# Attention with the split probabilities as stationary operands and v with columns of ones moving

## The chip, the cores and the metric

The kernel runs on one NeuronCore of a Trainium2 chip. The metric is the time of one execution on the device in microseconds (us); lower is better. The kernel before takes 1997.43 us, the median of three runs (1996.18 to 1998.01).

## What is computed

A trunk of two residual layers over 1,024 tokens of width 1,024, in 4-byte floats. Layer 0 has two attention groups of 8 heads each, layer 1 one of 16:

```python
for i in range(DEPTH):                       # DEPTH = 2
    u = rms_norm(h, norm_g[i])
    if i % 2 == 0:                           # mla: 8 heads, q and k of 96, v of 64; chk: 8 heads of 64
        o_a = mla_attention(...)             # block-causal softmax over chunks of 64
        o_b = chunk_rel_attention(...)       # own chunk and 8 before it, with a position bias
        mixed = concat([o_a * silu(g_a), o_b * silu(g_b)]) @ ab_w_out
    else:                                    # fox: 16 heads of 64
        o_c = forgetting_attention(...)      # causal softmax with a cumulative forget bias
        mixed = (o_c * silu(g_c)) @ fox_w_out
    h = h + mixed
    h = h + (p[i] @ pe_w[i]) * sigmoid(rms_norm(h, pe_gate_norm[i]) @ pe_gate_w[i])
```

Every attention is `softmax(q k^T * scale + mask or bias) @ v`, per head.

## The kernel before

The program is a chain of stages with a barrier between them: `stage_ab` (norms, projections), `stage_attention` three times (mla, chk, then after `stage_oe("m")` fox), `stage_oe("t")` at the end. Stages hand data over through DRAM (`s_q`, `s_v`, `s_g` and others); the attention stages leave their gated outputs in SBUF as `a_hi` and `a_lo`, features on partitions. A value is kept as a sum of two parts of reduced precision (`hi`, `lo`, type fp32r), and a product is computed as hi·hi + hi·lo + lo·hi.

In `stage_attention` a head has NT = 8 query tiles of 128, and a tile t looks at key blocks `lowest(t)` to t, that is t + 1 blocks, in chk at most 5. The five instruction streams are written out by hand, in steps s = 8 · head + t:

- TensorE, step s: `score(s)` fills one of two PSUM areas (two matmul terms per piece of up to 512 keys, three in mla; a mask is added by a small bf16 matmul); `times_v` for a *pair* of query tiles, half of it in an even and half in an odd step; `turn_p(s - 2)` transposes the probabilities of tile s - 2 in pieces of up to 4 blocks, two pieces in flight; in even steps `spread_sums`, two transposes that bring 1/sum onto all partitions.
- ScalarE: `exp(s)` with the row sum in `accum_out`; `evacuate(s - 2)` copies each transposed piece to `pt_hi`; `take_far` copies P·v and the inverses out of PSUM.
- VectorE: `row_max(s)` (in chk bias and maximum in one custom operation); `invert`; `evacuate(s - 2)` computes `pt_lo`; `take_o` adds the half of P·v that stands on its own 64 partitions to the half in `far`.
- GpSimd: gate and inverse multiplied in (`gi`, `o`) and `a_lo` split, three operations of 1,024 columns per pair of heads; for the last pair VectorE does them.
- The DMA queue of SyncE: q, k, their low parts, v and the gate, a head ahead, each load of q and k whole.

In P·v a block of v is stationary (L1050): a head's 128 columns of v are [hi | lo] or, in odd heads, [lo | hi], and `pt_hi`, then `pt_lo` move, 256 columns of them where both tiles of the pair see the block:

```python
cols = slice(P, 2 * P) if j == 2 * u + 1 else slice(0, P) if j < lo1 else slice(0, 2 * P)
ins = nc.tensor.matmul(pv[:, uu % 2, 0, cols], v[:, b, j, :], part[:, u % 2, j - lo0, cols],
                       start=(m == 0), stop=(m == len(terms) - 1))
```

The first score term uses all 128 rows of the array (96 in mla). The second (L1009) uses `XROWS`: 64 in chk, 67 in fox (three rows carry the forget bias), 96 in mla.

The gate projection (units "g" in `stage_ab` L652 and `stage_oe("m")` L1595) has the weights stationary and 512 tokens moving, 24 matmuls per unit, 16 units in each stage; all other projections have tokens stationary and 256 weight columns moving.

Of the kernel before, what the change touches and what calls it, by code (L numbers as in the profile page):

```python
# [55 lines left out]
def build(nc, x, p, positions, norm_g, ab_w_in, mla_q_norm, mla_w_uq, mla_kv_norm, mla_w_ukv,  # L56
# [12 lines left out]
    s_g = dram("s_g", [FH, 64, S])  # L69
# [5 lines left out]
    f_g = dram("f_g", [FH, 64, S])  # L75
# [122 lines left out]
    def stage_ab():  # L198
        with ExitStack() as st:
# [86 lines left out]
            for u, (kind, c, n) in enumerate(units):  # L286
# [9 lines left out]
                if kind == "qk":  # L296
                    steps.append(("b", u))
# [67 lines left out]
            pair_g = s_g.rearrange("(c h) q n -> c (h q) n", h=2)  # L365

            with nc.Block() as block:

                @block.sync
                def _(sync):  # L370
# [39 lines left out]
                    for what, n in steps:  # L410
# [11 lines left out]
                        if what == "e" and ("e", n) in outs_at:  # L422
# [10 lines left out]
                            else:  # L433
                                m = c - G0
                                pair = (4 + 2 * m if m < 2 else 2 * m - 4) + t // 2
                                store(o, pair_g[pair, :, (t % 2) * HALF:(t % 2 + 1) * HALF], src[:, 0:HALF])
# [19 lines left out]
                def _(act):  # L456
# [20 lines left out]
                    def evacuate(u):  # L477
# [3 lines left out]
                        if ("e", u) in outs_at:  # L481
# [7 lines left out]
                            if kind == "g":  # L489
                                nc.scalar.activation(staged[:, o % 4, 0:HALF], src[:, 0, :], ACT.Silu).then_inc(out_made, 1)  # L490
                                return
# [76 lines left out]
                def _(pe):  # L568
# [47 lines left out]
                    def unit(u, part):  # L616
# [16 lines left out]
                        elif kind == "qk":  # L633
# [11 lines left out]
                        elif kind == "v":  # L645
                            last = tokens(dst[:, 0:256], c, n, a_hi, a_lo, 0, 256)
                        else:
                            w_hi, w_lo = wt.halves(c)
                            block, cols = slice(n // 2 * P, (n // 2 + 1) * P), slice(n % 2 * HALF, (n % 2 + 1) * HALF)
                            for k in range(KD):  # L650
                                for w, a in ((w_hi, a_hi), (w_hi, a_lo), (w_lo, a_hi)):
                                    last = nc.tensor.matmul(dst, w[:, k, block], a[:, k, cols],  # L652
                                                            start=(k == 0 and w is w_hi and a is a_hi),
                                                            stop=(k == KD - 1 and w is w_lo))
# [219 lines left out]
    def stage_attention(kind, heads, first_pair, q_of, k_of, v_of, g_of, extra_of):  # L874
# [3 lines left out]
        NU = NT // 2  # L878
# [7 lines left out]
        def turned(t):  # L886
# [5 lines left out]
        BEFORE = [sum(len(turned(t)) for t in range(n)) for n in range(NT + 1)]  # L892

        def piece(s):

            return BEFORE[NT] * (s // NT) + BEFORE[s % NT]

        def in_units(rows):
            return rows.rearrange("q (u n) -> q u n", u=NU)

# [874 lines left out]
```

## Time and profile before

| | us |
|---|---|
| median of three runs | 1997.43 |
| the profiled execution | 1996.7 |
| its span, first to last instruction | 1994.9 |
| stage mla, first score to last split | 160.1 |
| stage chk | 167.2 |
| stage fox | 295.6 |

The profile is a record of one execution. For each engine it has the start and the duration of every instruction and what ended the idle time before it. Over the whole span TensorE is busy 1783.1 us in matmuls and 1637.5 us in loads of stationary operands (these two overlap), VectorE 955.8, ScalarE 827.3 and GpSimd 98.3 us. The end of a matmul is modelled, and one starts before the one ahead of it ends; so its cost in a stream is the distance from its start to the next start, and the duration says little. The granted clock (PEclk) is a share of TensorE's 2.4 GHz. In the rows, PE is a matmul, PEld a load of the stationary operand, DVE VectorE, ACT ScalarE, POOL GpSimd, SPq the DMA queue; `out<-in rows*columns` gives the tensors and the part of the array; L and a number is the line of the kernel. A row of a window has the stretch (from:to), its length, the busy us of each engine with its number of instructions (x), the granted clock, the share of the DMA engines and their GB/s.

### The profile page before, as it was taken

The numbers are of one execution on the slowest core, as the hardware profiler recorded it, in microseconds if no ns is written. First come the engines' busy times: TensorE is split into PE (matmuls) and PEld (weight loads), VectorE is DVE, ScalarE is ACT, GpSimd is POOL, SyncE is SP. The second block draws the span as 40 slices with busy tenths as digits, with TensorE's granted clock in tenths as the row PEclk, the third lists the DMA queues.
The fourth block names the chain that finished last, engine by engine and source line by source line (L and its number), as shares of the span: only waits on it lengthen the run. The fifth ranks groups of instructions, "written<-read, shape, count | busy, mean of one in ns | idle before, by whom it ended". The sixth has DMA issues, their size and how long they took to land. (4 is left out here: it accounts for less than half of the span.)

```text
span 1994.9 us, 31875 instructions
## 1 busy us (share of the span) xinstructions
PE 1783.1 (89%) x12720; PEld 1637.5 (82%) x12720; DVE 955.8 (48%) x1797; ACT 827.3 (41%) x1702; POOL 98.3 (5%) x55
## 2 busy tenths in 40 slices
PE   5999778988996996999989999999968988869998
PEld 5999767867884775999988999998757777769898
DVE  5454556105774665234345444331057777722631
ACT  4433234215773675123153332312157878711410
POOL 0000000000210111000000000000002112100000
PEclk9999989998996998999999999999989999989999
DMA  5054468416424551510123433453174555251111
GB/s 179 22 197 143 119 160 220 122 56 171 127 75 111 138 129 42 184 54 27 49 106 106 127 123 119 131 138 102 45 178 122 142 138 129 64 180 48 64 64 38
DMA packets 178372, 223.94 MB, mean 112 GB/s; under 512 B 12857, under 2 KB 148297, under 8 KB 178225
## 3 DMA queue, kind: packets, MB, share of 16 engines
q1 hardware_dynamic: 177152, 218.43, 38.1%
q0 software_dynamic: 640, 2.62, 0.4%
q8 instruction: 102, 1.67, 0.4%
q10 hardware_dynamic: 432, 0.85, 0.1%
q14 instruction: 46, 0.37, 0.1%
HBM read 150.34 MB, written 77.29 MB: 114 GB/s over the span
## 5 line engine op out<-in xcount | busy, mean ns | idle before, releaser
L1562 PE MATMUL m_acc<-m_w_hi,g_a_hi 128*128 128x256 f32 (+1 forms) x1280 | 370.6, 290 | 19.0 <-DVE m_w_lo L179 14.6
L1562 PE MATMUL m_acc<-m_w_hi,g_a_lo 128*128 128x256 f32 (+1 forms) x1280 | 365.5, 286 | 0.0
L1562 PE MATMUL m_acc<-m_w_lo,g_a_hi 128*128 128x256 f32 (+1 forms) x1280 | 364.6, 285 | 0.0
L1562 PEld LDWEIGHTS m_acc<-m_w_hi,g_a_hi 128*128 128x128 f32 x1280 | 246.0, 192 | 19.4 <-DVE m_w_lo L179 14.7
L1562 PEld LDWEIGHTS m_acc<-m_w_lo,g_a_hi 128*128 128x128 f32 x1280 | 246.8, 193 | 0.0
L1562 PEld LDWEIGHTS m_acc<-m_w_hi,g_a_lo 128*128 128x128 f32 x1280 | 244.6, 191 | 0.0
L611 PE MATMUL pa_acc<-pa_w_hi,g_a_hi 128*128 128x256 f32 (+2 forms) x512 | 156.4, 305 | 15.9 <-DVE pa_w_lo L179 15.9
L1562 PE MATMUL t_acc<-t_w_hi,g_a_hi 128*128 128x256 f32 x512 | 146.9, 287 | 15.2 <-DVE t_w_lo L179 15.2
L611 PE MATMUL pa_acc<-pa_w_hi,g_a_lo 128*128 128x256 f32 (+2 forms) x512 | 151.8, 297 | 0.0
L611 PE MATMUL pa_acc<-pa_w_lo,g_a_hi 128*128 128x256 f32 (+2 forms) x512 | 151.5, 296 | 0.0
L1562 PE MATMUL t_acc<-t_w_hi,g_a_lo 128*128 128x256 f32 x512 | 145.6, 284 | 0.0
L1562 PE MATMUL t_acc<-t_w_lo,g_a_hi 128*128 128x256 f32 x512 | 144.9, 283 | 0.0
L1150 DVE TENSOR_TENSOR fox_pt_lo<-fox_turn,fox_pt_hi 128x128 fp32r<-128x128 f32 (+2 forms) x192 | 100.3, 550 | 59.5 <-ACT fox_pt_hi L1086 58.2
L1024 PE MATMUL fox_turn<-g_ident,fox_prob 128*128 128x128 f32 x576 | 90.8, 280 | 31.1 <-DVE fox_pt_lo L1150 29.9
L611 PEld LDWEIGHTS pa_acc<-pa_w_hi,g_a_hi 128*128 128x128 f32 x512 | 99.6, 195 | 16.4 <-issue 16.4
L1562 PEld LDWEIGHTS t_acc<-t_w_hi,g_a_hi 128*128 128x128 f32 x512 | 97.7, 191 | 15.3 <-DVE t_w_lo L179 15.3
L1086 ACT ACTIVATE fox_pt_hi<-fox_turn 128x128 fp32r<-128x128 f32 (+2 forms) x192 | 87.2, 489 | 47.5 <-PE fox_turn L1024 45.3
L1136 DVE TENSOR_REDUCE fox_neg_max<-fox_scores 128x1 f32<-128x128 f32 (+7 forms) x128 | 95.6, 747 | 17.1 <-PE fox_scores L1009 16.4
L1075 ACT ACTIVATE fox_prob<-fox_scores,fox_neg_max 128x128 f32<-128x128 f32 (+7 forms) x128 | 94.8, 741 | 20.1 <-DVE fox_neg_max L1136 20.0
L611 PEld LDWEIGHTS pa_acc<-pa_w_lo,g_a_hi 128*128 128x128 f32 x512 | 100.0, 195 | 0.0
L611 PEld LDWEIGHTS pa_acc<-pa_w_hi,g_a_lo 128*128 128x128 f32 x512 | 99.0, 193 | 0.0
L1562 PEld LDWEIGHTS t_acc<-t_w_lo,g_a_hi 128*128 128x128 f32 x512 | 98.4, 192 | 0.0
(284 smaller groups left out, 4136.4 us busy)
## 6 DMA issues: line engine op xcount, KB each, us to landing
m_w_raw<-in_fox_w_in SPq DMA_DIRECT2D x16, 1024.0 KB, 6.0
pa_w_raw<-in_ab_w_in SPq DMA_DIRECT2D x10, 1024.0 KB, 5.6
f_v<-m_pr SPq DMA_DIRECT2D x32, 256.0 KB, 2.8
fox_q<-f_q SPq DMA_DIRECT2D x32, 256.0 KB
fox_k<-f_k SPq DMA_DIRECT2D x32, 256.0 KB
fox_v<-f_v SPq DMA_DIRECT2D x16, 512.0 KB, 3.3
s_mq<-pa_xr SPq DMA_DIRECT2D x32, 192.0 KB, 3.0
s_mk<-pa_xr SPq DMA_DIRECT2D x32, 192.0 KB, 3.1
```

What stands on the lines that cost most here:

```text
L611: last = nc.tensor.matmul(dst, a[:, k, t * P:(t + 1) * P], w[:, k, n0:n0 + n], start=(k == 0 and a is m_hi and w is w_hi), stop=(k == kt - ...
L1024: last = nc.tensor.transpose(turn[:, g % 2, m, :], prob[:, s % 3, (j - lo) * P:(j - lo + 1) * P], ident[:])
L1075: nc.scalar.activation(prob[:, s % 3, 0:n], src, ACT.Exp, bias=neg_max[:, s % 4:s % 4 + 1], scale=-1.0 if chk else 1.0, accum_out=total[:, ...
L1086: nc.scalar.activation(pt_hi[:, u % 2, at:at + len(js), (s % 2) * P:(s % 2 + 1) * P], turn[:, g % 2, 0:len(js), :], ACT.Copy).then_inc(pt_ ...
L1136: nc.vector.tensor_reduce(r, scores[:, t % 2, 0:n], AX_X, ALU.max, negate=True).then_inc(maxed, 1)
L1150: nc.vector.tensor_tensor(pt_lo[where], turn[:, g % 2, 0:len(js), :], pt_hi[where].bitcast(F32), ALU.subtract).then_inc(pt_lo_done, 1)
L1562: last = nc.tensor.matmul(dst, a[:, k, t * P:(t + 1) * P], w[:, k0 + k, 0:n], start=(k == 0 and a is m_hi and w is w_hi), stop=(k == kt - ...
```

## The change

The roles in P·v are swapped. A transposed block of probabilities (`pt_hi`, then `pt_lo`) is stationary, and v moves: 130 columns [lo | hi | 1 1] against `pt_hi`, 66 columns [hi | 1 1] against `pt_lo`. Each query tile is a unit of its own, and P·v comes out with queries on partitions, with the row sum in column 128. VectorE inverts that sum and takes the outputs, scaled; GpSimd adds the two halves and multiplies by the gate for four tiles at once; TensorE turns the outputs by four transposes per half of a head pair, and ScalarE and VectorE split them into `a_hi` and `a_lo` from PSUM. The spreading of sums, `accum_out` and `far` go.

With it come: gates with tokens on partitions (`s_g`, `f_g`), so that the gate projection has tokens stationary and is done in two parts of 256 columns like the others; the second score term over all 128 rows in chk and fox, with zeros that GpSimd fills in at the start of the stage; v loaded into rows of 130; the first head's q and k loaded in two halves of the tokens, v between them; PSUM areas chosen by s instead of t. The core of the diff ("..." marks what is left out):

```diff
-    s_g = dram("s_g", [FH, 64, S])
+    s_g = dram("s_g", [KD, P, ST, P])
...
-        return blocks[:, :, 1:3, :] if small else blocks[:, :, 0::3, :]
+        return blocks[:, :, 0::2, :] if small else blocks[:, :, 1::2, :]
...
-                if kind == "qk":
+                if kind in ("qk", "g"):
                     steps.append(("b", u))
...
-                        elif kind == "qk":
+                        elif kind in ("qk", "g"):
                             last = tokens(dst[:, part * 256:(part + 1) * 256], c, 2 * n + part, a_hi, a_lo, 0, 256)
...
-                            for k in range(KD):
-                                for w, a in ((w_hi, a_hi), (w_hi, a_lo), (w_lo, a_hi)):
-                                    last = nc.tensor.matmul(dst, w[:, k, block], a[:, k, cols],
...
-            XROWS = QK if mla else 67 if fox else 64
+            VCOLS = P + 2
...
-            v = sp.sb("v", [P, 2, ST, P], F32R)
-            gate = sp.sb("gate", [P, 2, S])
-            gi = sp.sb("gi", [P, S])
-            far = sp.sb("far", [P, 2, NU, 2, 2 * P])
+            v = sp.sb("v", [P, 2, ST, VCOLS], F32R)
+            gate = sp.sb("gate", [P, 2, ST, P])
+            o_parts = sp.sb("o_parts", [P, 2, ST, 2, 64])
+            o_sum = sp.sb("o_sum", [P, 4, 64])
+            pt_hi = sp.sb("pt_hi", [P, 3, WIDE // P, P], F32R)
+            pt_lo = sp.sb("pt_lo", [P, 3, WIDE // P, P], F32R)
...
+                        if hd == 0:
+                            load_v(0)
+                            load_qk(0, slice(HALF, S), in_rest)
...
+                        if s == NT // 2:
+                            pe.wait_ge(in_rest, 16 * QKDMA)
...
-                                ins = nc.tensor.matmul(dst, a[0:r, b, rows], kk[0:r, b, keys], start=(m == 0),
+                                ins = nc.tensor.matmul(dst, a[0:KROWS, b, rows], kk[0:KROWS, b, keys], start=(m == 0),
...
+                    def turn_o(g):
+                        _, m, half = ring[g]
+                        pe.wait_ge(gated, 4 * m + 2 + half + 1)
+                        turn_ready(g)
+                        for n in range(4):
+                            last = nc.tensor.transpose(turn[:, g % 2, n, :], o[:, m % 2, 4 * half + n, :], ident[:])
...
-                    def spread_sums(uu):
...
+                        wait(pe, taken, s - 1)
+                        pe.wait_ge(pt_lo_done, p_upto[s])
+                        for j in range(lo, t + 1):
+                            nc.tensor.matmul(pv[:, s % 2, 0:VCOLS], pt_hi[:, s % 3, j - lo, :], v[:, b, j, :],
+                                             start=(j == lo), stop=False)
+                            ins = nc.tensor.matmul(pv[:, s % 2, 64:VCOLS], pt_lo[:, s % 3, j - lo, :], v[:, b, j, 64:VCOLS],
+                                                   start=False, stop=(j == t))
...
+                    for s in steps:
                         if s < TILES:
                             score(s)
+                        for g in turns_at[s]:
+                            if ring[g][0] == "p":
+                                turn_p(g)
+                            else:
+                                turn_o(g)
+                        if 0 <= s - 3 < TILES:
+                            times_v(s - 3)
...
-                                             scale=-1.0 if chk else 1.0,
-                                             accum_out=total[:, s // 2 % 4, s % 2:s % 2 + 1]).then_inc(exped, 1)
+                                             scale=-1.0 if chk else 1.0).then_inc(exped, 1)
...
-                    def take_far(uu):
...
+                    def invert(s):
+                        dve.wait_ge(pv_done, s + 1)
+                        wait(dve, taken, s - 3)
+                        nc.vector.reciprocal(inverse[:, s % 4:s % 4 + 1], pv[:, s % 2, P:P + 1]).then_inc(inverted, 1)
+
+                    def take(s):
...
+                        nc.vector.tensor_scalar(o_parts[:, hd % 2, t].rearrange("q a n -> q (a n)"), pv[:, s % 2, 0:P],
+                                                inverse[:, s % 4:s % 4 + 1], None, ALU.mult).then_inc(taken, 1)
...
+                    for s in steps:
+                        if 0 <= s - 4 < TILES:
+                            invert(s - 4)
                         if s < TILES:
                             row_max(s)
+                        for g in turns_at[s]:
...
+                        if 0 <= s - 4 < TILES:
+                            take(s - 4)
...
+                    if not mla:
+                        pool.memset(qx[64:P, :, :].bitcast(F32), 0.0).then_inc(q_filled, 1)
+                    if fox:
+                        pool.memset(kx[64:P, :, :].bitcast(F32), 0.0).then_inc(k_filled, 1)
+                        pool.wait_ge(q_filled, 1)
+                        pool.memset(qx[64:67, :, :].bitcast(F32), 1.0).then_inc(q_filled, 1)
+                    for n in range(2 * heads):
...
+                        nc.gpsimd.tensor_tensor(o_sum[:], o_parts[:, b, tiles, 0, :], o_parts[:, b, tiles, 1, :], ALU.add)\
+                            .then_inc(added, 1)
...
+                        nc.gpsimd.tensor_tensor(o[:, m % 2, tiles, cols], o_sum[:], gate[:, m % 2, tiles, cols], ALU.mult)\
+                            .then_inc(gated, 1)
```

## Rows read from the trace of the kernel before

**Rows 1.** Windows mla, chk, fox: length, busy PE PEld DVE ACT POOL, clock, DMA.

```profile
454.90:614.97 160.07, 144.71 (x1024) 125.62 (x1024) 115.30 (x227) 113.44 (x260) 21.47 (x9) 0.97 0.37 106
624.58:791.80 167.22, 151.71 (x880) 120.75 (x880) 103.03 (x291) 104.80 (x260) 21.37 (x9) 0.88 0.42 107
1459.50:1755.10 295.60, 256.66 (x1856) 217.76 (x1856) 221.29 (x451) 228.48 (x520) 49.96 (x21) 0.98 0.50 123
```

**Rows 2.** Windows, the same columns: 512-column, then 256-column matmuls.

```profile
385.00:440.00 55.00, 55.00 (x237) 44.20 (x236) 2.60 (x2) 7.78 (x11) 0.00 (x0) 1.00 0.20 67
950.00:1005.00 55.00, 55.00 (x462) 55.00 (x462) 15.33 (x16) 6.86 (x10) 0.00 (x0) 1.00 0.15 44
```

**Rows 3.** Timeline of TensorE in chk: start us, duration us, then the instruction.

```profile
730.02 0.40 PE L1009 MATMUL chk_scores<-chk_k,chk_q 128*128 128x512 f32 x1
730.27 0.20 PE L1013 MATMUL chk_scores<-g_low_q,g_ident_b 128*128 128x64 bf16 x1
730.40 0.49 PE L1009 MATMUL chk_scores<-chk_k,chk_qx 64*128 64x512 f32 x1
730.82 0.39 PE L1050 MATMUL chk_pv<-chk_pt_hi,chk_v 128*128 128x256 f32 x1
...
731.34 0.27 PE L1050 MATMUL chk_pv<-chk_pt_hi,chk_v 128*128 128x128 f32 x1
731.45 0.27 PE L1050 MATMUL chk_pv<-chk_pt_lo,chk_v 128*128 128x128 f32 x1
```

**Rows 4.** Timeline of ScalarE: tile 0 of two heads each, mla, chk, fox.

```profile
474.00 0.37 ACT L1075 ACTIVATE mla_prob<-mla_scores,mla_neg_max 128x128 f32<-128x128 f32 x1
...
585.10 0.37 ACT L1075 ACTIVATE mla_prob<-mla_scores,mla_neg_max 128x128 f32<-128x128 f32 x1
...
668.69 0.40 ACT L1075 ACTIVATE chk_prob<-chk_prob,chk_neg_max 128x128 f32<-128x128 f32 x1
...
762.03 0.40 ACT L1075 ACTIVATE chk_prob<-chk_prob,chk_neg_max 128x128 f32<-128x128 f32 x1
...
1476.38 0.37 ACT L1075 ACTIVATE fox_prob<-fox_scores,fox_neg_max 128x128 f32<-128x128 f32 x1
...
1726.03 0.37 ACT L1075 ACTIVATE fox_prob<-fox_scores,fox_neg_max 128x128 f32<-128x128 f32 x1
```

**Rows 5.** Page, costliest groups: busy us, mean ns, idle before it, releaser.

```profile
L1024 PE MATMUL fox_turn<-g_ident,fox_prob 128*128 128x128 f32 x576 | 90.8, 280 | 31.1 <-DVE fox_pt_lo L1150 29.9
```

**Rows 6.** Groups by shape, same columns: VectorE, and one of ScalarE.

```profile
L1158 DVE TENSOR_TENSOR fox_o<-fox_pv,fox_far 64x256 f32<-64x256 f32 x64 | 26.7, 417 | 3.3 <-ACT fox_far L1096 2.4
...
L1150 DVE TENSOR_TENSOR fox_pt_lo<-fox_turn,fox_pt_hi 128x256 fp32r<-128x256 f32 x32 | 13.4, 419 | 10.0 <-ACT fox_pt_hi L1086 9.9
...
L1136 DVE TENSOR_REDUCE fox_neg_max<-fox_scores 128x1 f32<-128x512 f32 x16 | 10.9, 683 | 5.3 <-PE fox_scores L1009 5.3
...
L1141 DVE RECIPROCAL fox_inverse<-fox_total 128x2 f32<-128x2 f32 x64 | 10.0, 156 | 0.9
...
L1150 DVE TENSOR_TENSOR fox_pt_lo<-fox_turn,fox_pt_hi 128x128 fp32r<-128x128 f32 x16 | 4.7, 291 | 8.2 <-ACT fox_pt_hi L1086 7.4
...
L1096 ACT ACTIVATE fox_far<-fox_pv 64x512 f32<-64x512 f32 x64 | 37.9, 591 | 4.0 <-PE fox_pv L1050 2.4
```

**Rows 7.** Timeline of TensorE in fox, as above.

```profile
1498.86 0.48 PE L1009 MATMUL fox_scores<-fox_kx,fox_qx 67*128 67x512 f32 x1
1499.17 0.28 PE L1050 MATMUL fox_pv<-fox_pt_hi,fox_v 128*128 128x256 f32 x1
```

**Rows 8.** Timeline, the start of mla: first DMA issue and first score.

```profile
446.16 0.34 SPq L949 DMA_DIRECT2D mla_q<-s_mq  x1
...
454.89 0.29 PEld L1009 LDWEIGHTS mla_scores<-mla_k,mla_q 96*128 96x128 f32 x1 [12.92 <-DMA mla_kx<-s_mk]
```

**Rows 9.** Timeline, the end of mla: last P·v matmul and last split.

```profile
608.68 0.28 PE L1050 MATMUL mla_pv<-mla_pt_lo,mla_v 128*128 128x128 f32 x1
...
613.75 1.23 DVE L1181 TENSOR_TENSOR g_a_lo<-mla_o,g_a_hi 128x1024 fp32r<-128x1024 f32 x1 [1.12 <-ACT g_a_hi L1104]
```

More of the change, by code:

```diff
@@ L890, in turned @@
             return [js[n:n + cut] for n in range(0, len(js), cut)]
[L892 to L899, printed above, removed]
+        steps = range(TILES + 7)
+        turns_at = {s: [] for s in steps}
+        ring = []
+        p_of, o_of = {}, {}
+        p_upto, ring_upto = [], []
+        for s in steps:
+            if 0 <= s - 2 < TILES:
+                for js in pieces_of((s - 2) % NT):
+                    turns_at[s].append(len(ring))
+                    p_of[len(ring)] = len(p_of)
+                    ring.append(("p", s - 2, js))
+                p_upto.append(len(p_of))
+                ring_upto.append(len(ring))
+            done = s - 6
+            if done >= 0 and done // NT % 2 == 1 and done % NT in (3, NT - 1):
+                turns_at[s].append(len(ring))
+                o_of[len(ring)] = len(o_of)
+                ring.append(("o", done // NT // 2, done % NT // 4))
+        o_turned = {ring[g][1:]: g + 1 for g in o_of}
         with ExitStack() as st:
@@ L986, in score @@
                             pe.wait_ge(in_qk[b], 16 * QKDMA * (hd // 2 + 1))
-                            if fox and hd < 2:
-                                pe.wait_ge(ones, 1)
+                            if hd < 1 and not mla:
+                                pe.wait_ge(q_filled, 2 if fox else 1)
+                        if s == NT // 2:
+                            pe.wait_ge(in_rest, 16 * QKDMA)
                         wait(pe, maxed if chk else exped, s - 1)
@@ L1111, in _ @@
+                    for s in steps:
+                        for g in turns_at[s]:
+                            if g in p_of:
+                                copy_p(g)
+                            else:
+                                give(g)
                         if s < TILES:
                             exp(s)
[L1113 to L1116 removed]
@@ L1133, in row_max @@
                             return
-                        if s >= 4:
-                            dve.wait_ge(exped, s - 3)
-                        nc.vector.tensor_reduce(r, scores[:, t % 2, 0:n], AX_X, ALU.max, negate=True).then_inc(maxed, 1)
-                    def invert(uu):
-                        dve.wait_ge(exped, 2 * uu + 2)
-                        wait(dve, spread, uu - 3)
-                        nc.vector.reciprocal(inverse[:, uu % 4, :], total[:, uu % 4, :]).then_inc(inverted, 1)
@@ L1587, in unit @@
                                 return
[L1588 removed]
+                        else:
                             last = tokens(dst[:, 0:table[c][1]], c, n, a_hi, a_lo, 0, KD, table[c][1])
[L1590 to L1597 removed]
                         last.then_inc(summed, 1)
```

315 lines of the change are left out of this document (128 added, 187 removed).

## The prediction

> **What bounds the kernel now.** I read the windows of the three attention stages first, then the start times of single matmuls, then the rows of vector and scalar work, last the edges of a stage. The stages mla, chk and fox take 160, 167 and 296 us, and TensorE is busy for 145, 152 and 257 of them, far more than any other engine [rows 1]. But the busy times of matmuls overlap, so a busy TensorE is not a full one; what a matmul costs I take from the distance between starts.
>
> - A matmul that moves 256 columns with a stationary block of its own: 55 us hold 462, 0.12 us each. One that moves 512: 237 in 55 us, 0.232 us each [rows 2].
> - One that moves 128 columns and loads its own block: from 731.34 to 731.45, 0.11 us [rows 3]. It moves half the columns of the first kind and takes nearly as long, so there the load of the block sets the pace, not the columns. This is the number on which everything turns.
>
> The change touches these 623 us and the gate projection of two other stages. Per head, from the first exp of one head to that of another (heads 1 and 7, 2 and 7, 1 and 15): mla (585.10 - 474.00)/6 = 18.5 us, chk (762.03 - 668.69)/5 = 18.7, fox (1726.03 - 1476.38)/14 = 17.8 [rows 4].
>
> What TensorE must do per head, at those rates (36 key blocks over the eight query tiles; chk has 30):
> fox: scores 9,216 columns and narrow pieces 4.6, 36 transposes 4.0, 8 transposes that spread the sums 0.9, P·v 32 of 256 columns 3.8 and 8 narrow ones 0.7, and 0.6 explained below: 14.6 us. So 3.2 of the 17.8 are waits, mostly short; the trace shows one kind, transposes waiting for the low half of the probabilities, 31.1 us in fox [rows 5].
> mla: scores have three terms, 7.2, and no 0.6: 16.6, waits 1.9.
> chk: scores 8.3 (below), transposes 3.3, spreading 0.9, P·v 24 of 256 columns and 12 narrow 4.0: 16.5, waits 2.2.
> TensorE is thus the engine with the most work in all three. VectorE has 115.30/8 = 14.4, 12.9 and 13.8 us per head, ScalarE much the same [rows 1].
>
> **P·v with probabilities stationary.** A pair of query tiles shared its v block before; now each (tile, key block) has two matmuls of 130 and 66 columns, each with its own load. 72 per head instead of 40. At the narrow rate 72 x 0.11 = 7.9 us against 4.5: +3.4 in mla and fox; chk 60 x 0.11 = 6.6 against 4.0: +2.6. The 130 and 66 columns are not in the trace; bounds are 0.11 [rows 3] and 0.12 [rows 2], and I take 0.11. The Trainium skill, "TensorE: Matmul & The Clock Gate", section "Back-to-back issue gap", gives about 81 ns for a sustained pair of load and matmul at 128 columns; by that P·v would cost 5.8 us per head instead of 7.9. The rows show 110 ns for these 4-byte operands, and the rows decide.
>
> **The sums.** Spreading them (8 transposes, -0.9) goes, since the columns of ones give the sum with the queries on partitions. Four transposes of outputs per head come (+0.4). Gone from ScalarE are the 0.59 us copy of each pair of tiles (`far`) [rows 6], -2.4 us per head, and the read of the accumulator after each exp, which I leave unpriced: with 14 us per head now ScalarE falls behind both others as the engine in charge.
>
> **Rows of the array.** This is the gain. In chk the second score term reads 64 rows and its neighbours 128. A 512-column one started at 730.40 and the next matmul at 730.82, 0.42 us instead of 0.232; a 64-column mask before it took 0.13 (730.27 to 730.40), where its columns are worth 64/512 of 0.232, 0.03 us [rows 3]. That is 0.19 + 0.10 for each of 12 such terms per head, 3.5 us, and I add 0.5 for narrow first terms, which are late for the same reason: chk's scores cost 8.3 us where full rows would cost 4.3, -4.0 per head. In fox the term has 67 rows; the matmul after it starts 0.31 us later (1498.86 to 1499.17) [rows 7], 0.08 more than 0.232; eight times per head that is the 0.6. The change pads both with zeros to 128 rows. mla keeps its 96. That the loss comes from the switch of row count and goes with it is my reading of these rows; the bounds are all of it and nothing.
>
> TensorE after, per head: fox 4.6 + 4.0 + 7.9 + 0.4 = 16.9 (+2.3); mla 7.2 + 4.0 + 7.9 + 0.4 = 19.5 (+2.9); chk 4.3 + 3.3 + 6.6 + 0.4 = 14.6 (-1.9).
>
> **VectorE.** It loses 4 sums of outputs (0.42) and 4 reciprocals (0.16) per head, and gets 8 reciprocals, 8 scaled copies of 128 columns and one 512-column split of outputs that GpSimd did. A 128-column operation out of PSUM is 0.29 at most and more than the reciprocal's 0.16 [rows 6]; I take 0.27. -2.3 + 1.3 + 2.2 + 0.7 = +1.9: 15.7 in fox, 16.3 in mla, 14.8 in chk. In chk it overtakes TensorE; in fox it paces the narrow tiles. Per step in fox (scores of tile t, transposes of t-2, P·v of t-3) TensorE has 0.5 + 0.2 + 0.2 = 0.9 us at t = 3 and VectorE a maximum of 512 columns 0.68, a split of 256 0.42, 0.16 and 0.27, 1.5 us [rows 6]; at t = 4 and 5 they are nearly level. About 0.6 us per head that TensorE must wait.
>
> **Waits.** New: P·v waits until the outputs two tiles back are taken; behind it stand the next scores. `invert` stands ahead of the row maximum and waits for P·v of four tiles back, which in TensorE's queue is ahead of those scores; no cost. The longer P·v hides part of what the transposes wait for. Waits today are 3.2, 1.9 and 2.2. I take 2.3 for fox (0.6 pacing and 1.7 latency), 1.5 for mla and 2.7 for chk (VectorE paces it). Periods: fox 19.2 (+1.4), mla 21.0 (+2.5), chk 17.3 (-1.4). Over 16, 8 and 8 heads: +22, +20, -11 us.
>
> **Cold start.** The clock is not always granted in full: chk has 0.88 over its stage, the others 0.97 and 0.98 [rows 1], a mix of 2.4 and 1.2 GHz. Of 160, 296 and 167 us that is 10, 12 and 40 us at the low level. More matmuls there in mla and fox, some 3 us, fewer in chk, some -2: +1.
>
> **GpSimd.** Its operations of 21.47/9 = 2.4 us, three per pair [rows 1], become eight of a quarter the size; a step lies between them and the transposes that wait for them. Nothing. The fills at a stage's start are 2,048 columns each, one in chk, three in a row in fox, and the first scores and the last small load wait for them. At that rate one is 4.8 us; a fill reads nothing, and I take 2: over about when the loads land, nothing. At 4.8 us fox would start 5 us later than now; that stays in the range.
>
> **Gate projection.** Tokens become stationary: 768 matmuls of 256 columns for 384 of 512, in each of two stages. 768 x 0.119 - 384 x 0.232 = 2.3 us each [rows 2]; +4 in all, bounds 0 and 5. ScalarE's copy only changes its order of columns. v goes into rows of 130, so its packets are 512 bytes; its load is issued a head ahead. Nothing.
>
> **Edges.** mla's first DMA is issued at 446.16, the first score starts at 454.89, held by the last of four loads [rows 8]. Now half of each is waited for. Half of 8.7 us would be 4.4; 0 if tile 4 then waits for the rest. I take 2.7 in each stage: -8 (0 to -13). The end: from the last P·v matmul at 608.68 to the end of the last split, 613.75 + 1.23 = 614.98, 6.3 us [rows 9]. Now reciprocal 0.16, copy 0.27, two GpSimd operations 1.2, transposes 0.7, ScalarE 0.6, VectorE 0.7 and hand-overs 0.8: 4.4. Over three stages -6 (-9 to 0).
>
> **Sum.** 22 + 20 - 11 + 1 + 4 - 8 - 6 = +22 us on the profiled 1996.7 us (span 1994.9), 0.7 us below the median of 1997.4. Forecast: 2019 us, 1.1% slower.
>
> **Rivals.**
> *The waits vanish* (faster). If the longer P·v covers half of the waits, leaving 1.1, 0.8 and 1.9, the periods are 18.0, 20.3 and 16.5: +3 + 14 - 18, with the rest -9, is -10: 1987; with still less waiting 1970. For it: the transposes wait for work that runs beside P·v. Against: VectorE gets more, not less, and in the narrow steps there is nothing to hide behind. It wins once fox waits under 1.5 us per head. Chance 0.30.
> *The waits stay.* VectorE's longer queue delays the low halves as much as P·v covers: 3.2, 1.9 and 3.0 give +37 + 23 - 9 - 9 = +42: 2039. Chance 0.14.
> *The clock falls.* P·v moves 98 columns per load where it moved up to 256. If mla and fox were granted 0.88 like chk [rows 1], a tenth of their 455 us goes: +45 on the forecast, 2064. The same page of the Trainium skill, Part 1, says the clock follows how busy the array is; whether loads count as busy no row here shows. Against it: TensorE will idle less. Chance 0.06.
> *Loads come faster than the narrow rate.* The 0.11 us was seen where every matmul moved 128 columns; half of the new ones move 66. At 0.08 us P·v would save 2.1 us per head in fox and mla and 1.8 in chk; half of that would show beside VectorE, (24 x 2.1 + 8 x 1.8)/2 = 32: 1987. No row shows a rate under 0.11. Chance 0.03. The page's 81 ns would be this case.
> The forecast itself has 0.47.
>
> **Range and chances.** Low 1980 (the first rival but its tail), high 2046 (the second with full costs of the edges). A measurement of this kernel tells 0.2%, 4 us. Faster: 0.26 of the first rival and 0.03: 0.29. Same: 0.04 of it and 0.05 of the forecast: 0.09. Slower: the rest, 0.62. The forecast's own range is 2003 to 2034.
>
> **What would show it.** P·v matmuls start 0.11 us apart: right; nearer 0.08 or 0.2: the main term is wrong. After chk's second term the next matmul starts 0.23 us later: the padding works. Periods of 19.2, 21.0 and 17.3 us. VectorE 15 to 16 us busy per head. First scores 6 us after the first DMA instead of 8.7. Granted clock of fox at 0.97 or more.

## The result and the profile after

The changed kernel takes 2026.3 us (median of four runs, 2015 to 2055) against 1996.8 for the kernel before on the same chip: a ratio of 1.0135, 95% interval 1.0084 to 1.0187. The ratios leave out runs more than 1.5% above the fastest of their kernel, here the one of 2055 us. Run again beside the experiments it gave 1.0151 (1.0104 to 1.0197). The forecast was 2019 us. The profiled execution of after took 2029.5 us, 32.8 us more than that of before.

Windows of the stages mla, chk and fox, now each from the first DMA issue of a stage to the end of its last split, first of before, then of after; columns as in [rows 1].

```profile
446.16:614.97 168.81, 144.72 (x1024) 125.63 (x1024) 115.30 (x227) 114.73 (x261) 21.47 (x9) 0.95 0.40 113
615.77:791.81 176.04, 151.71 (x880) 120.75 (x880) 103.03 (x291) 104.80 (x260) 21.37 (x9) 0.86 0.44 111
1449.43:1755.14 305.71, 256.68 (x1856) 217.78 (x1856) 223.09 (x452) 229.76 (x521) 49.96 (x21) 0.97 0.52 125
```

```profile
447.75:628.67 180.92, 167.18 (x1248) 150.69 (x1248) 123.39 (x297) 94.46 (x169) 23.34 (x32) 0.95 0.38 106
629.49:807.61 178.12, 162.83 (x1040) 144.43 (x1040) 111.87 (x361) 83.32 (x168) 25.18 (x33) 0.76 0.44 110
1468.18:1787.21 319.03, 299.15 (x2304) 270.10 (x2304) 241.79 (x593) 187.44 (x337) 52.01 (x67) 0.95 0.50 120
```

mla is 12.1 us longer, chk 2.1, fox 13.3. The rest came between the stages: 1.6 us before mla, 2.9 between chk and fox, 0.7 after fox. chk, where the gain was to be, is longer too, and its granted clock is 0.76 where it was 0.86.

Timeline of ScalarE in after, the exps of tile 0 as in [rows 4]: two heads of mla, two of chk, two of fox.

```profile
534.94 0.37 ACT L1094 ACTIVATE mla_prob<-mla_scores,mla_neg_max 128x128 f32<-128x128 f32 x1
556.52 0.37 ACT L1094 ACTIVATE mla_prob<-mla_scores,mla_neg_max 128x128 f32<-128x128 f32 x1
576.02 0.37 ACT L1094 ACTIVATE mla_prob<-mla_scores,mla_neg_max 128x128 f32<-128x128 f32 x1
...
716.15 0.41 ACT L1094 ACTIVATE chk_prob<-chk_prob,chk_neg_max 128x128 f32<-128x128 f32 x1
...
781.79 0.40 ACT L1094 ACTIVATE chk_prob<-chk_prob,chk_neg_max 128x128 f32<-128x128 f32 x1
...
1585.45 0.37 ACT L1094 ACTIVATE fox_prob<-fox_scores,fox_neg_max 128x128 f32<-128x128 f32 x1
1605.07 0.37 ACT L1094 ACTIVATE fox_prob<-fox_scores,fox_neg_max 128x128 f32<-128x128 f32 x1
1622.54 0.37 ACT L1094 ACTIVATE fox_prob<-fox_scores,fox_neg_max 128x128 f32<-128x128 f32 x1
```

Heads now come in two lengths. In fox one takes 19.62 us and the next 17.47, in mla 21.58 and 19.50; before they were within 0.3 us of each other in both stages. chk's last four take (781.79 - 716.15)/4 = 16.4 us, against 18.7 in [rows 4]. The long head is the one after each pair, where the outputs of the pair's first half are transposed.

Timeline of TensorE in after, at that place in fox.

```profile
1586.24 0.37 PE L1026 MATMUL fox_scores<-fox_kx,fox_qx 128*128 128x256 f32 x1
1586.45 1.04 PE L1046 MATMUL fox_turn<-g_ident,fox_prob 128*128 128x128 f32 x8
1588.55 0.63 PE L1055 MATMUL fox_turn<-g_ident,fox_o 128*128 128x128 f32 x4 [1.07 <-DVE fox_pt_lo L1145]
1588.94 0.31 PE L1068 MATMUL fox_pv<-fox_v,fox_pt_hi 128*128 128x130 f32 x1
1589.09 0.25 PE L1070 MATMUL fox_pv<-fox_v,fox_pt_lo 128*128 128x66 f32 x1
1589.16 0.31 PE L1068 MATMUL fox_pv<-fox_v,fox_pt_hi 128*128 128x130 f32 x1
```

Eight transposes of tile 7's probabilities, two pieces, fill both `turn` buffers; 8 x 0.11 later, at 1587.33, the outputs' transposes are next in the queue and start at 1588.55. They need the buffer of the first piece, and ScalarE and VectorE are not through with it. A P·v pair of two matmuls takes 1589.16 - 1588.94 = 0.22 us.

The two groups of transposes in fox, by shape, columns as in [rows 5].

```profile
L1046 PE MATMUL fox_turn<-g_ident,fox_prob 128*128 128x128 f32 x576 | 87.0, 279 | 0.2 <-DVE fox_pt_lo L1145 0.2
...
L1055 PE MATMUL fox_turn<-g_ident,fox_o 128*128 128x128 f32 x64 | 10.4, 286 | 10.8 <-DVE fox_pt_lo L1145 8.5 <-POOL fox_o L1204 2.2
```

The 31.1 us of [rows 5] are gone: TensorE no longer waits for the low halves at the probabilities' transposes. What is left of that wait stands at the outputs' transposes, once per pair of heads.

Windows of after: chk's first three heads, its other five, and a stretch of fox.

```profile
636.60:711.70 75.10, 72.61 (x316) 64.03 (x316) 36.49 (x112) 27.04 (x55) 5.83 (x8) 0.50 0.47 111
711.70:799.60 87.90, 84.76 (x695) 75.95 (x695) 72.29 (x240) 54.96 (x112) 16.10 (x22) 1.00 0.44 112
1739.10:1749.30 10.20, 10.20 (x44) 8.93 (x43) 4.52 (x14) 3.02 (x6) 1.45 (x2) 0.50 0.17 51
```

For 75 us chk ran at 1.2 GHz, though TensorE was busy for 72.61 of them; its first three heads, from an exp at 636.48 to the one at 716.15, took 80 us, where three at 2.4 GHz take 49 (3 x 16.4).

### The profile page after: what moved, and what is told of

Same layout as the page of the kernel before. It is cut to its first block and busy times, and to the rows that moved or that the text cites. A ratio compares the mean times of both kernels' runs of the same rounds, so it can differ in the third digit from the quotient of the medians.

```text
span 2027.7 us, 35470 instructions
## 1 busy us (share of the span) xinstructions
PE 1864.0 (92%) x14320; PEld 1779.2 (88%) x14320; DVE 991.5 (49%) x2078; ACT 743.5 (37%) x1334; POOL 106.1 (5%) x148
## 5 line engine op out<-in xcount | busy, mean ns | idle before, releaser
L1571 PE MATMUL m_acc<-m_w_hi,g_a_hi 128*128 128x256 f32 (+1 forms) x1536 | 443.4, 289 | 15.1 <-DVE m_w_lo L179 10.6
L1571 PE MATMUL m_acc<-m_w_hi,g_a_lo 128*128 128x256 f32 (+1 forms) x1536 | 437.2, 285 | 0.0
L1571 PE MATMUL m_acc<-m_w_lo,g_a_hi 128*128 128x256 f32 (+1 forms) x1536 | 437.2, 285 | 0.0
L1571 PEld LDWEIGHTS m_acc<-m_w_hi,g_a_hi 128*128 128x128 f32 x1536 | 294.0, 191 | 15.7 <-DVE m_w_lo L179 11.0
L613 PE MATMUL pa_acc<-pa_w_hi,g_a_hi 128*128 128x256 f32 (+2 forms) x768 | 229.7, 299 | 21.3 <-DVE pa_w_lo L179 21.3
L613 PE MATMUL pa_acc<-pa_w_hi,g_a_lo 128*128 128x256 f32 (+2 forms) x768 | 224.7, 293 | 0.0
L613 PE MATMUL pa_acc<-pa_w_lo,g_a_hi 128*128 128x256 f32 (+2 forms) x768 | 223.6, 291 | 0.0
L1068 PE MATMUL fox_pv<-fox_v,fox_pt_hi 128*128 128x130 f32 x576 | 142.6, 312 | 0.2 <-DVE fox_o_parts L1165 0.2
L1070 PE MATMUL fox_pv<-fox_v,fox_pt_lo 128*128 128x66 f32 x576 | 133.5, 249 | 0.0
L1068 PEld LDWEIGHTS fox_pv<-fox_v,fox_pt_hi 128*128 128x128 f32 x576 | 112.6, 196 | 2.5 <-DVE fox_o_parts L1165 0.3
L1070 PEld LDWEIGHTS fox_pv<-fox_v,fox_pt_lo 128*128 128x128 f32 x576 | 112.8, 196 | 0.0
```

The costliest lines, as they stand in the source:

```text
L613: last = nc.tensor.matmul(dst, a[:, k, t * P:(t + 1) * P], w[:, k, n0:n0 + n], start=(k == 0 and a is m_hi and w is w_hi), stop=(k == kt - ...
L1068: nc.tensor.matmul(pv[:, s % 2, 0:VCOLS], pt_hi[:, s % 3, j - lo, :], v[:, b, j, :], start=(j == lo), stop=False)
L1070: ins = nc.tensor.matmul(pv[:, s % 2, 64:VCOLS], pt_lo[:, s % 3, j - lo, :], v[:, b, j, 64:VCOLS], start=False, stop=(j == t))
L1571: last = nc.tensor.matmul(dst, a[:, k, t * P:(t + 1) * P], w[:, k0 + k, 0:n], start=(k == 0 and a is m_hi and w is w_hi), stop=(k == kt - ...
```

## The experiments

My theory after the comparison had three parts: a wait at the ring of transpose buffers that I had missed; a padding whose gain is real; and a clock that the new kernel holds less well. The rivals were that the added work itself (VectorE, GpSimd, more columns) costs the time, and that the padding does little. Ratios are against the kernel before, run beside on the same chip. The experiments ran on three chips: e0, e1, e2 and e3 on one, e5, e6, e7 and e9 on a second, e10, e11 and e12 on a third. Profiles are of one execution each. Microsecond differences between kernels are worked out from the ratios.

**The ring.** e1 moves the outputs' transposes of the first half one step on.

```diff
-            done = s - 6
-            if done >= 0 and done // NT % 2 == 1 and done % NT in (3, NT - 1):
+            for done, last in ((s - 7, 3), (s - 6, NT - 1)):
+                if done >= 0 and done // NT % 2 == 1 and done % NT == last:
...
```

> The changed kernel with one edit: the four transposes of outputs that close the first half of a pair of heads come one step of the loop later, behind the single narrow piece of tile 0 of the next head, instead of right behind the two pieces of tile 7. Theory 'the ring waits': the transposes of outputs share the two transpose buffers with the probabilities, and in the old place their buffer is the first piece of tile 7, transposed in the same step, so TensorE waits for ScalarE's copy and VectorE's split of it, about 2.1 us once per pair of heads. Then 16 pairs x 2.1 = 34 us go: 0.983 of the changed kernel, fox's pairs from 37.1 to about 35 us, mla's from 41.1 to 39, chk's warm ones from 32.8 to 31. Rival 'it is only the added work': what costs is that VectorE and GpSimd have more to do, and a wait taken away here comes back in the next step; 0 to -8 us. Rival 'GpSimd': TensorE waits there for the gated outputs, which come 2 us later by nature; then one step later also saves, but fewer than 34 us, and the row of the outputs' transposes would have named GpSimd.

> The changed kernel itself once more, on the chip of the runs beside it, so that they can be set against it. Expected: 1.0135 of the kernel before (its interval was 1.008 to 1.019), that is +27 us.

e1: 1.0019 (0.9988 to 1.0050); after itself, e0: 1.0151. Timeline of e1: TensorE at the moved place, then the exps of tile 0 in fox.

```profile
1555.58 0.42 PE L1026 MATMUL fox_scores<-fox_kx,fox_qx 128*128 128x384 f32 x1
1555.84 0.27 PE L1046 MATMUL fox_turn<-g_ident,fox_prob 128*128 128x128 f32 x1
1555.95 0.60 PE L1055 MATMUL fox_turn<-g_ident,fox_o 128*128 128x128 f32 x4
```

```profile
1551.92 0.37 ACT L1094 ACTIVATE fox_prob<-fox_scores,fox_neg_max 128x128 f32<-128x128 f32 x1
1570.28 0.37 ACT L1094 ACTIVATE fox_prob<-fox_scores,fox_neg_max 128x128 f32<-128x128 f32 x1
1587.74 0.37 ACT L1094 ACTIVATE fox_prob<-fox_scores,fox_neg_max 128x128 f32<-128x128 f32 x1
```

The outputs' transposes start 0.11 us after the one before them, with no wait. The long head of fox falls from 19.62 to 18.36, the short one stays at 17.47: 1.26 us per pair, not the 2.1 I expected. The 2.1 had held the 8 x 0.11 of the outputs' own transposes, which stay; they are all of the 0.9 between the two heads now. 16 pairs x 1.3 = 21 us of the 26 that the time shows. (The wait was a little longer in chk: its long head falls from 17.55 to 16.09.) The other rivals fall: the wait didn't come back in the next step, and GpSimd wasn't it. The 5 us beyond the 21 are inside the two intervals; they may be clock, for the profiled chk of e1 has 0.91 where after's has 0.76, but that is not shown. Without this wait the changed kernel takes the same time as the kernel before.

**The columns of P·v.** In e3 the low matmul moves all 130 columns, `pt_lo` times the whole of `v`.

```diff
-nc.tensor.matmul(pv[:, s % 2, 64:VCOLS], pt_lo[...], v[:, b, j, 64:VCOLS],
+nc.tensor.matmul(pv[:, s % 2, 0:VCOLS], pt_lo[...], v[:, b, j, :],
```

> The changed kernel, but the matmuls of the low half of the probabilities move all 130 columns of v instead of 66 (also adds the product of the two low halves, which the kernel leaves out). Theory 'the load sets the pace': a P.v matmul costs 0.11 us whether it moves 66 or 130 columns, so the pair stays at 0.223 us and the time at 0 to +2 us. Rival 'columns count': the pair is 143 ns behind the 130-column one and 80 ns behind the 66-column one; if 64 columns more cost 64/512 of 0.232 = 29 ns each, 36 x 24 + 30 x 8 = 1104 pairs give +32 us (1.6%).

e3: 1.0061 (1.0026 to 1.0095), 18 us faster than after, which neither theory had. Timeline of TensorE in e3, a P·v in fox.

```profile
1555.15 0.27 PE L1070 MATMUL fox_pv<-fox_v,fox_pt_lo 128*128 128x130 f32 x1
1555.26 0.28 PE L1068 MATMUL fox_pv<-fox_v,fox_pt_hi 128*128 128x130 f32 x1
1555.37 0.28 PE L1070 MATMUL fox_pv<-fox_v,fox_pt_lo 128*128 128x130 f32 x1
```

0.11 us apart again: 64 columns more cost nothing, and the load sets the pace. Heads at full clock are as in after, 17.45 and 19.61 in fox. So the gain is in the clock: over the runs that count in the ratios e3 was granted 0.956 in the mean (ten runs), after with e0 0.946 (seven), before 0.957. The edit also evens out the spacing, 0.11 and 0.11 us where it was 0.15 and 0.07, and adds the product of the two low halves; no run parts these from the columns. e10 asks whether it adds to e1's gain; it holds both edits.

> The changed kernel with the outputs' transposes of the first half one step later and with all 130 columns moved by the low matmuls too. Moving more columns had made the kernel faster (1.0151 to 1.0061 of the kernel before) at the same periods at full clock. Theory 'columns bring the clock back': the gain was clock alone, chk at 1.2 GHz for 24 us instead of 79 to 85, and it adds to that of the later transposes, which ran at 0.936 to 0.957 of the clock: all runs near 0.96, 0.990 to 0.995 of the kernel before, and the spread between runs (1983 to 2023) shrinks. Rival 'one cause': the later transposes already remove what the columns helped against, 1.000 to 1.003 with the same spread.

e10: 0.9945 (0.9914 to 0.9977), mean clock 0.956 in eight runs, e1's 0.949 in ten. The two gains add as far as the intervals tell: those of e1 and e10 lie 0.001 apart, on different chips. In both pairs the kernel that moved more columns in the same time was granted more clock. The spread shrank little (1975 to 2006, e1's was 1983 to 2023), and e10's profile has chk at 0.85, lower than e1's 0.91: columns don't decide in one execution when the clock comes back.

**Which engine paces a head.** e11 leaves out the matmuls of `pt_lo`; the low half is still made and waited for.

```diff
-ins = nc.tensor.matmul(pv[:, s % 2, 64:VCOLS], pt_lo[:, s % 3, j - lo, :], v[:, b, j, 64:VCOLS],
-                       start=False, stop=(j == t))
...
```

> The changed kernel without the matmuls of the low half of the probabilities (that term of the product is left out; the low half is still made and waited for, so that only TensorE's work is less). It is to tell which engine paces the changed kernel's heads. Theory 'TensorE has no waits left': by the sum of its work it needs 17.5 us per head in fox and 19.5 in mla, which are the measured periods; without 36 x 0.11 = 4.0 us it falls under VectorE's 15.7 to 16.3, which takes over: periods at full clock of 15.7 to 16.7 in fox and 16.3 to 17.5 in mla, 1 to 3 us less. Rival 'VectorE or the hand-overs pace the steps': periods at full clock of 17.2 to 17.5 and 19 to 19.5, hardly less. The time as a whole says little, since the clock may fall with less work.

e11: 0.9689 (0.9649 to 0.9729), two runs. Timeline of e11, exps of tile 0 in mla and fox.

```profile
510.54 0.37 ACT L1092 ACTIVATE mla_prob<-mla_scores,mla_neg_max 128x128 f32<-128x128 f32 x1
527.20 0.37 ACT L1092 ACTIVATE mla_prob<-mla_scores,mla_neg_max 128x128 f32<-128x128 f32 x1
545.82 0.37 ACT L1092 ACTIVATE mla_prob<-mla_scores,mla_neg_max 128x128 f32<-128x128 f32 x1
...
1584.01 0.37 ACT L1092 ACTIVATE fox_prob<-fox_scores,fox_neg_max 128x128 f32<-128x128 f32 x1
1601.62 0.37 ACT L1092 ACTIVATE fox_prob<-fox_scores,fox_neg_max 128x128 f32<-128x128 f32 x1
1617.11 0.37 ACT L1092 ACTIVATE fox_prob<-fox_scores,fox_neg_max 128x128 f32<-128x128 f32 x1
```

Short heads fall from 19.50 to 16.66 in mla and from 17.47 to 15.49 in fox. With 36 x 0.11 = 4.0 us less to do, TensorE gives 2.8 and 2.0 back; then it waits for others: in fox the transposes of the probabilities now wait for VectorE's low halves again (6.5 us from 1470 to 1660 in e11, against 0.2 in the whole of fox in after). So TensorE paced the changed kernel's heads and VectorE didn't.

**The padding.** e2 undoes it alone (the first diff), e7 puts it alone, and in chk only, into the kernel before (the second), e9 is e2 with a warm start (below).

```diff
+            XROWS = QK if mla else 67 if fox else 64
...
+                                r = KROWS if m == 0 else XROWS
...
```

```diff
-            XROWS = QK if mla else 67 if fox else 64
+            XROWS = QK if mla else 67 if fox else P
...
+                    if chk:
+                        pool.memset(qx[64:P, :, :].bitcast(F32), 0.0).then_inc(ones, 1)
```

> The changed kernel with the padding alone undone: the second score term again reads 64 rows of the array in chk and 67 in fox. The time only; the rows left out hold zeros. Theory of the prediction: a change of row count costs; chk gets slower by 4.0 us per head (32 us), fox by 0.6 (10 us), mla by nothing. Rival 'only to half': the trace of the changed kernel has 0.317 us after a 512-column second term in chk, where the prediction had 0.232 and the kernel before 0.428, so the loss per term is 0.11 and 0.09 for a mask behind it, 12 terms per head: 2.4 us per head, 19 us. Rival for fox: the 0.085 us between a 512-column term and what follows is there with 128 rows too, so 67 rows cost nothing: 0.

> The kernel before with chk's padding alone: the second score term reads 128 rows, of which 64 hold zeros, filled once by GpSimd. Prediction's theory: 4.0 us per head of TensorE's work go, but VectorE (12.9 us busy of 18.7) then paces part of it; if the waits stay as they are, chk's periods fall from 18.7 to about 15.5 and the time by 25 us, 0.987. Rival 'half': the switch costs 0.11 per term, as the changed kernel's trace shows, 2.4 us per head: -19 us, 0.990. Rival 'the clock': in the changed kernel with the 64 rows put back chk stayed at the low clock for its whole 286 us; so rows decide the clock too, and here the falls of 3.4 us (three in chk) and some of the 37 us at its start go as well: up to 20 us more, 0.980.

e2: 1.0753 (1.0710 to 1.0795), 120 us slower than after, nearly three times the 42 I expected at most. e7: 0.9872 (0.9854 to 0.9890), 26 us faster than before. Window of chk, whole, in e2; then chk in e7 with two exps of tile 0.

```profile
630.02:916.17 286.15, 271.39 (x1040) 221.53 (x1040) 117.66 (x361) 82.57 (x168) 25.01 (x33) 0.50 0.29 68
```

```profile
630.60:750.00 119.40, 105.22 (x825) 90.45 (x824) 89.39 (x266) 98.36 (x242) 21.53 (x9) 1.00 0.54 137
...
640.62 0.40 ACT L1075 ACTIVATE chk_prob<-chk_prob,chk_neg_max 128x128 f32<-128x128 f32 x1
...
736.45 0.40 ACT L1075 ACTIVATE chk_prob<-chk_prob,chk_neg_max 128x128 f32<-128x128 f32 x1
```

With 64 rows and the new P·v, chk never left 1.2 GHz; with 128 rows and the old P·v it was at 2.4 GHz from 630.60 on and its heads took (736.45 - 640.62)/6 = 16.0 us instead of 18.7. That is the padding's gain, rate and clock together: in before those heads were granted 0.95 to 0.96, so about 0.8 of the 2.7 us (half of the time at 1.2 GHz, an estimate) is clock and 1.9 rate. Over the whole stage the clock was 0.50 with 64 rows and the new P·v (e2), 0.86 with 64 and the old (before), 0.76 with 128 and the new (after), 0.95 with 128 and the old (e7). In fox e2 shows no rate: its heads at full clock are 17.49 and 19.63 with 67 rows, 17.47 and 19.62 with 128. In e7 fox is untouched.

> The changed kernel with the padding undone and the 16 matmuls at the start of each stage. Undoing the padding alone cost 120 us, and chk ran at 1.2 GHz throughout, 34.2 us per head instead of 16.4. This run is to tell the rate from the clock. Theory 'it only could not get up': entered at full clock, chk holds it, and its heads take 16.4 + 2.4 to 16.4 + 4.0 us, 19 to 20.4: 90 us less than without the warm start. Rival 'it cannot hold it': with 64-row terms the clock falls again within a head or two and stays down: 34 us per head, at most 15 us less.

e9: 1.0895 (1.0858 to 1.0932), worse than e2. Windows of chk and fox, whole, in e9.

```profile
637.81:922.75 284.94, 275.22 (x1056) 224.99 (x1056) 117.62 (x361) 82.80 (x168) 24.99 (x33) 0.51 0.28 69
1584.26:1940.68 356.42, 339.10 (x2320) 305.16 (x2320) 245.14 (x593) 187.48 (x337) 52.09 (x67) 0.86 0.45 108
```

Its chk was granted 1.00 of the clock from 645.03 to 650, in its first head, 0.51 in the next 5 us, and stayed at 1.2 GHz, 34.2 us per head. So it isn't the start alone: chk with 64 rows and this P·v doesn't hold the clock, or get it back. What makes e9 worse than e2 is not chk, which is as long in both (285 and 286 us), but fox: 356 us at 0.86 of the clock, in e2 324 at 0.93, in after 319 at 0.95. Whether the 67 rows cost clock there is open; these are single executions.

**A warm start.** e5 adds 16 matmuls at TensorE's start of each attention stage, e6 puts them on e1.

```diff
+for _ in range(16):
+    nc.tensor.matmul(scores[:, 1, 0:HALF], a_hi[:, 0, 0:P], a_hi[:, 0, 0:HALF], start=True, stop=True)
```

> The changed kernel with 16 matmuls of 512 columns put at TensorE's start of each attention stage, while the first loads are awaited; their results are overwritten by the second tile's scores. Theory 'the slow start keeps the clock low': the clock falls in the pause between two stages, and chk's first three heads run at 1.2 GHz (28 us each) because the engine enters them slow; with TensorE busy before, the clock is full at or soon after the first score, chk's first three heads take 49 to 52 us instead of 80 and mla's and fox's first heads 4 to 5 us less: -25 to -38 us against the changed kernel, 0.997 to 1.003 of the kernel before. Rival 'chk's own work keeps it low': the clock is low or falls again in chk's first heads whatever came before them; mla and fox gain 4 to 5 us each and chk nothing: -10 us. Third: if the 16 matmuls end after the loads, the first scores come up to 2 us later in each stage.

> Both edits at once: the outputs' transposes of the first half one step later, and the 16 matmuls at the start of each attention stage. If the two are independent the gains add: the later transposes gave 26 us (1.0151 to 1.0019 of the kernel before), the warm start should give some 10 us where chk starts well already and 28 where it doesn't: 0.985 to 0.995 of the kernel before. Rival 'the later transposes already give the clock back': in that run chk was at the low clock for 26 us only, so that 1 to 3 us in each stage are left: 0.997 to 1.002.

e5: 1.0272 (1.0226 to 1.0318); e6: 0.9965 (0.9940 to 0.9991). The one is slower than after; the other is a little faster than e1, but their intervals touch. e5 shows none of the 10 us or more that I expected, e6 lies by its rival's range (0.997 to 1.002), and the sign is open. Windows of e5 in chk: the end of the added matmuls, then the heads behind them.

```profile
644.80:648.30 3.50, 3.17 (x16) 2.26 (x14) 0.64 (x4) 0.30 (x1) 0.00 (x0) 0.94 0.92 276
652.00:679.00 27.00, 26.34 (x118) 23.93 (x118) 12.31 (x38) 8.78 (x18) 1.45 (x2) 0.50 0.66 154
```

The clock was full as the scores began and was lost again in the first head. There the tiles are narrow and the DMA engines still busy (0.66); which of the two matters, if either, no run shows. So the pause between the stages isn't all that keeps it low.

**The starts.** e12 is e7 with the first head's q and k loaded in two halves, as in the change.

```diff
+                        if hd == 0:
+                            load_qk(0, slice(0, HALF), in_qk[0])
...
+                            load_qk(0, slice(HALF, S), in_rest)
```

> The kernel before with chk's padding (which alone gave 0.9872) and, from the change, the first head's loads of q and k in two halves, so that the first scores of a stage wait for half of them. The changed kernel's first scores came 5.5, 5.4 and 6.2 us after the first DMA instead of 8.7, 8.8 and 10.1. Theory 'the starts count in full': 3.2 + 3.4 + 3.9 = 10 us less than with the padding alone, 0.982. Rival 'tile 4 waits for the rest': the gain is given back at the fifth tile of the first head, 0 to -3 us, 0.986 to 0.987.

e12: 0.9859 (0.9832 to 0.9887), the fastest of the kernels that compute the whole product, but not told apart from e7. Timeline of TensorE in e12, the start of fox.

```profile
1424.29 0.48 PE L1017 MATMUL fox_scores<-fox_k,fox_q 128*128 128x128 f32 x1 [9.86 <-DMA fox_kx<-s_cum]
...
1429.86 0.79 PE L1017 MATMUL fox_scores<-fox_k,fox_q 128*128 128x512 f32 x1 [0.88 <-DMA fox_kx<-s_cum]
```

The first score comes 6.0 us after the first DMA instead of 9.9, and then tile 4 waits for the other half. The stage is 304.25 us long with halves and 305.51 without; mla 167.21 and 169.87, chk 146.62 and 145.64. Of 10 us 3 are left, by single executions. The changed kernel has the same wait, at the 512-column score of tile 4 in chk and fox:

```profile
641.40 0.79 PE L1026 MATMUL chk_scores<-chk_k,chk_q 128*128 128x512 f32 x1 [1.65 <-DMA chk_qx<-s_q]
...
1480.42 0.79 PE L1026 MATMUL fox_scores<-fox_k,fox_q 128*128 128x512 f32 x1 [1.23 <-DMA fox_kx<-s_cum]
```

## Why the prediction was right, and where it was not

The time came out 7 us from the forecast and the sign was right, but that is largely luck: wrong terms met in the sum. The heads were forecast at +22 + 20 - 11 = +31 us. At full clock they measured 16 x 0.7 + 8 x 2.0 - 8 x 2.3 = +9, and that already holds 21 us of a wait that the forecast didn't have. The clock, forecast at +1, took up to 26. P·v's loads cost TensorE what was forecast, but by themselves they don't carry the sign: e1, without the wait, takes the time of the kernel before, and e10, which moves more columns as well, is at 0.9945, some 1985 us. That is where the rival *the waits vanish* stood, 1987. Term by term:

- **P·v.** 0.11 us apart forecast, 0.111 measured, at 66 and at 130 columns (e3). Right (the cost before is 0.2 too low in the sum: 32 x 0.12 + 8 x 0.11 is 4.7, not 4.5, and 24 x 0.12 + 12 x 0.11 is 4.2, not 4.0). The rival of faster loads is out: a matmul that moved 130 columns was followed 0.15 us later, one that moved 66 only 0.07 later, and the pair is 0.22 us (the timeline of after above).
- **TensorE's work per head.** mla 19.5 forecast, 19.50 the short head. fox 16.9 forecast, 17.47 measured; the 0.6 between them is a step that failed. I had read the 0.08 us after a 67-row term [rows 7] as a cost of the row count that goes with the padding. It stays: with 128 rows a matmul of another kind still starts 0.31 us after a 512-column second term (1601.19 to 1601.50 in the trace of after), and e2 has the same heads at 67 rows. Why is open.
- **Waits.** I kept 2.3, 1.5 and 2.7 us per head. In the short heads there are practically none: of the 31.1 us in [rows 5] 0.2 are left. The mechanism of the rival *the waits vanish* was the true one. The work behind P·v did not slow the low halves.
- **The ring.** Missed altogether. I wrote of the outputs' transposes that they add 0.4 us of work and that a step lies between them and GpSimd. The step was there; what I didn't ask was whose buffer they take. Right behind a tile of two pieces it is one that was filled in the same step. 1.3 us per pair, 21 us in all (e1).
- **Periods.** Forecast 19.2, 21.0, 17.3; measured 18.55, 20.54, and 16.4 in chk at full clock. Against before that is +0.7, +2.0 and -2.3 where I had +1.4, +2.5 and -1.4; about 0.8 of chk's 2.3 is clock that its heads lacked before.
- **Rows of the array.** Timeline of TensorE in after: the scores of a chk tile with padded rows, to be set beside [rows 3].

```profile
770.28 0.48 PE L1026 MATMUL chk_scores<-chk_k,chk_q 128*128 128x512 f32 x1
770.61 0.20 PE L1030 MATMUL chk_scores<-g_low_q,g_ident_b 128*128 128x64 bf16 x1
770.65 0.48 PE L1026 MATMUL chk_scores<-chk_k,chk_qx 128*128 128x512 f32 x1
770.97 0.38 PE L1046 MATMUL chk_turn<-g_ident,chk_prob 128*128 128x128 f32 x2
```

  The next matmul starts 0.32 us after the padded term; it was 0.42 before and 0.232 in the forecast. First term, mask and second term together take 0.69 us against 0.80 (730.02 to 730.82), so 0.11 less where I claimed 0.19 + 0.10. By the heads of e7 the rate gave 1.9 us per head, half of my 4.0. The padding's whole gain of 26 us still came near my 4.0 x 8 = 32 because it gave chk its clock too: chk is 30 us shorter in e7 (145.64 against 176.04), and its time at 1.2 GHz falls from 49 to 15 us. The mechanism that I had was half of it; the size was luck. The Trainium skill, "TensorE: Matmul & The Clock Gate", section "Step-by-step: what each phase is for", says that the time of a load goes with its columns and that the row count doesn't matter. The trace of before agrees for the load itself: the 64-row loads of chk's second term take 201 ns in the mean, the 128-row loads of its first 211. What the short term costs stands between the starts of matmuls.
- **Clock.** I had +1 us for the low level and 0.06 for a fall. From the windows above, 2 x (1 - clock) x length is the time at 1.2 GHz: 17 + 49 + 18 = 84 us before, 18 + 86 + 32 = 136 after. If half of such time is lost, the 52 us more cost up to 26. The rival *the clock falls* had the cause (fewer columns per load), but put it in mla and fox in full; it came in chk, in single stretches of fox (the 10.2 us above), and in other executions of the same kernel also in mla, whose window had 0.78 in e0's profile. That the columns bear on it is what e3 and e10 speak for, with the reservation above on the spacing. Why chk stays low so long in one execution and not in another is open.
- **VectorE.** 15.7, 16.3 and 14.8 us busy per head forecast; 241.79/16 = 15.1, 15.4 and 14.0 measured. It didn't pace the heads (e11).
- **Gate projection.** +4 forecast, +4.5 in the stretches that hold it (1.6 and 2.9). No run has it alone, but it fits.
- **Starts.** The first scores come 3.2, 3.4 and 3.9 us earlier, more than the 2.7 I took. The upper bound of 0, "if tile 4 then waits for the rest", was the better guess: e12 keeps 3 of 10.
- **Tails.** 6.3 to 4.9 us in mla, by 1.4 for a forecast 1.9.

So the change as a whole costs 30 us (1.0151). Of that the ring is 21 to 26 (e1) and the clock that more columns give back 15 to 18 (e10 against e1, e3 against after). The padding in chk saves 26 us in the kernel before (e7), but undoing it in the changed kernel costs 120 (e2), so its worth depends on the P·v beside it, and the parts can't simply be added. What P·v's loads and the gate projection cost by themselves, no run has alone. The kernel before with the padding alone beats both kernels; with the split loads as well it is at 0.986.

## What to carry over

Before new work is put into a ring of buffers, ask at each place where it enters whose buffer it takes and when that one was filled; a place one step later can be free. When a loop is paced by loads of the stationary operand, fewer moved columns save no time, and here they went with less clock (e3, e10). A change made of several parts should be run in parts: here the padding alone was a gain (e7) and the rest hid it. And when a forecast comes out right, set each of its terms beside its measured one before trusting it: here the heads were 22 us too dear and the clock up to 25 too cheap.

## What I had not expected of the hardware

- A short-row term cost far more than its rate: with the new P·v, chk with 64-row terms ran its whole 286 us at 1.2 GHz in e2, and in e9 lost a clock that was full.
- TensorE can be busy 72.61 of 75.10 us and be granted 1.2 GHz all that time.
- Columns that the result doesn't need made a kernel faster: 1.0151 to 1.0061, and 1.0019 to 0.9945, with the same 0.22 us per pair of matmuls.
